# A hybrid decoder layer on one core: the first norm folded into the modulation rows, the sample output ahead of the routers, later ranks and normed rows behind the flags

## The reference, cut to what matters

```python
def hybrid_layer(x, c, ...):                     # 256 prompt tokens, and 8 x 8 sample tokens
    ada = jax.nn.silu(c) @ w_ada + b_ada
    shift1, scale1, gate1, shift2, scale2, gate2 = jnp.split(ada[:, None, :], 6, axis=-1)
    u = x * (1 + scale1) + shift1
    ...                                          # projection, attention or cache attention, short convolution
    mix = jnp.concatenate([attn, conv], axis=-1) @ w_o
    x = layer_norm(DEEPNORM_ALPHA * x + (1 + gate1) * mix, ln1_g, ln1_b)
    u2 = x * (1 + scale2) + shift2
    ffn = moe(u2, ...)                           # router on u2, top 4 of 32 experts, clamped SwiGLU
    x = layer_norm(DEEPNORM_ALPHA * x + (1 + gate2) * ffn, ln2_g, ln2_b)
```

## Time and profile before

| | us |
|---|---|
| median of three runs | 1467.15 (1466.29 to 1475.74) |
| the profiled execution's own time | 1470.0 |
| its span, first to last instruction | 1468.2 |
| PE busy, DVE busy, ACT busy in the span | 1390.4, 492.4, 243.8 |

### The profile page before, as it was taken

How to read it: one execution, slowest core, us unless ns; L and a number is a source line. 1 busy time by engine, 2 the same in 40 slices (tenths; PEclk the granted TensorE clock), 3 DMA queues, 4 the chain that set the end, 5 groups by cost and what they waited for, 6 DMA issues and landing times.

```text
span 1468.2 us, 21691 instructions
## 1 busy us (share of the span) xinstructions
PE 1390.4 (95%) x7813; PEld 574.1 (39%) x7814; DVE 492.4 (34%) x1098; ACT 243.8 (17%) x432; POOL 13.7 (1%) x22
## 2 busy tenths in 40 slices
PE   5999999999958999999999999999999999999993
PEld 2555666665432333333333333333333333333331
DVE  2211356554672222233223332223322322223336
ACT  0001334442010111111111111111111111111110
POOL 0000000000010000000000000000000000000000
PEclk9999999999968999999999999999999999999996
DMA  9949448999845889999999998999999999998941
GB/s 339 391 163 351 175 178 306 419 424 384 282 177 233 322 350 404 426 425 426 425 426 427 427 400 354 412 425 427 426 423 428 425 426 425 426 406 342 403 206 36
DMA packets 60900, 523.72 MB, mean 357 GB/s; under 512 B 8124, under 2 KB 8437, under 8 KB 20682
## 3 DMA queue, kind: packets, MB, share of 16 engines
q1 hardware_dynamic: 57696, 517.61, 86.0%
q0 software_dynamic: 1344, 4.90, 0.9%
q10 hardware_dynamic: 1834, 0.84, 0.3%
HBM read 519.87 MB, written 3.46 MB: 356 GB/s over the span
## 4 chain that ended last, share of the span: by engine, by line
PE 82%; DMA 10%; DVE 4%; issue 1%; SPq 1%; ACT 0%; DVEq 0%; ACTq 0%
PE ps L1679 29%; PE ps L1758 14%; PE ps L1280 6%; PE ps L1217 5%; PE ps L1584 5%; PE ps L1616 5%; DMA arena<-in_cache_v 4%; DMA arena<-in_w_up 4%; PE ps L1508 3%; DMA arena<-in_w_in 2%; PE ps L1671 2%; PE ps L1450 2%; PE ps L1277 2%; PE ps L1689 1%; PE ps L1607 1%
## 5 line engine op out<-in xcount | busy, mean ns | idle before, releaser
L1679 PE MATMUL ps<-arena 128*64 128x512 f32 x2048 | 450.5, 597 | 1.3 <-DMA arena<-in_w_up 1.2
L1679 PEld LDWEIGHTS ps<-arena 128*64 128x64 f32 x2048 | 144.3, 138 | 306.0 <-issue 302.4
L1758 PE MATMUL ps<-arena 128*64 128x512 f32 x1024 | 228.4, 599 | 2.4 <-issue 2.2
L1217 PE MATMUL ps<-arena 128*128 128x128 f32 (+4 forms) x1075 | 151.4, 282 | 30.9 <-DVEq L984 10.9
L1151 DVE TENSOR_SCALAR arena<-ps 128x512 f32<-128x512 f32 (+1 forms) x35 | 24.2, 692 | 417.6 <-PE ps L1679 356.4
L1217 PEld LDWEIGHTS ps<-arena 128*128 128x128 f32 (+4 forms) x1075 | 116.8, 144 | 94.1 <-issue 45.2
L1758 PEld LDWEIGHTS ps<-arena 128*64 128x64 f32 x1024 | 71.3, 138 | 153.8 <-issue 153.8
L1584 PE MATMUL ps<-arena 128*64 128x512 f32 (+1 forms) x396 | 97.5, 611 | 2.3 <-DVE arena L1092 2.3
L675 ACT ACTIVATE arena<-arena 128x512 f32<-128x512 f32 (+1 forms) x35 | 22.1, 631 | 446.5 <-DVE arena L1151 446.5
L1105 DVE TENSOR_TENSOR arena<-arena,ps 128x512 f32<-128x512 f32 x33 | 22.8, 690 | 196.3 <-PE ps L1607 196.0
L1280 PE MATMUL ps<-arena 128*128 128x320 f32 x288 | 85.0, 448 | 3.6 <-DMA arena<-in_w_in 3.6
(11 more groups left out here) (234 smaller groups left out, 900.9 us busy)
## 6 DMA issues: line engine op xcount, KB each, us to landing
arena<-in_w_up SPq DMA_DIRECT2D x128, 2048.0 KB, 15.2
arena<-in_w_down SPq DMA_DIRECT2D x128, 1024.0 KB, 12.7
arena<-in_w_ada SPq DMA_DIRECT2D x12, 2048.0 KB, 17.7
arena<-in_cache_k SPq DMA_DIRECT2D x16, 1536.0 KB, 14.3
arena<-in_cache_v SPq DMA_DIRECT2D x16, 1536.0 KB, 9.7
arena<-in_w_in SPq DMA_DIRECT2D x6, 2048.0 KB, 20.8
arena<-in_cache_k SPq DMA_DIRECT2D x32, 192.0 KB, 13.0
arena<-in_cache_v SPq DMA_DIRECT2D x32, 192.0 KB, 10.8
```

The costliest lines, as they stand in the source:

```text
L1217: return nc.tensor.transpose(o, i, ident[0:n, 0:n])
L1679: ins = mm(bank(part)[64 * h:64 * h + 64], xe_t[:, 0, at:at + 64], up_w[:, k, FF * part + 512 * h:FF * part + 512 * h + 512], start=False, ...
L1758: ins = mm(bank(3)[64 * h:64 * h + 64], a_t[:, 0, at:at + 64], dn_w[:, kk, 512 * h:512 * h + 512], start=kk == 0, stop=kk == KC - 1)
```

## The change

The first norm's gain and bias are multiplied into the modulation rows beforehand (`fold_norm`: shift2 + (1 + scale2) b, and (1 + scale2) g), for the prompt's rows ahead of `residual_sums(0)` and for the samples' behind `modulate(0)`. u2 then comes from the residual rows in two operations, through `mix`; the normed rows themselves are made by `keep_rows`, tiles 0 and 1 behind the flags, tile 2 behind the first `gathered_turned`. mod_s is loaded earlier, x for tile 2 later, the ln1 bias into the first eighth of w_down's place, whose last quarter to load now waits for `x1_kept`, as GpSimd's ln2 loads do; b_up is loaded after `wo_done` 3. `output_sample` stands ahead of router 0, the residual of tile 2 ahead of all routes, and the roots ahead of the exponentials on ScalarE. The gates are written by one operation. Ranks count from one (compared with `place`, which is iota + 1), and the later rounds' ranks are made behind the flags. Left out below: semaphore names, the places of `place`, `head_mask` and `query_sum`, and a separate bank for each tile's logits. Lines stand eight columns further left than in the file.

```diff
@@ -123,9 +122,7 @@
 MX = KTX + AC * NCACHE
-head_mask = view(MX, 256)
-query_sum = view(MX + 256, 3, 8)
-assert MX + 280 <= 24576
+assert MX <= 24576
@@ -213,7 +213,7 @@
 u2_t = view(R4 + 3 * D, KC, 128)
-ln1 = [view(R5, D), view(R2 + 2 * D, D)]
+ln1 = [view(R5, D), view(W + 16 * D, D)]
 xe_t = view(R4, 2, 512)
@@ -426,10 +427,10 @@
     sp.wait_ge(og_ready, 1)
-    for a, name in enumerate(("ln1_g", "ln1_b")):
-        sp.dma_start(ln1[a], t[name][0:1, :].to_broadcast([128, D])).then_inc(tail_in, 16)
+    sp.dma_start(ln1[0], t["ln1_g"][0:1, :].to_broadcast([128, D])).then_inc(ln1_in, 16)
     sp.wait_ge(vec_out, 64)
     sp.wait_ge(s_done, NB)
+    sp.dma_start(ln1[1], t["ln1_b"][0:1, :].to_broadcast([128, D])).then_inc(ln1_in, 16)
     sp.dma_start(mod_p, vectors[0:1, 0:3 * D].to_broadcast([128, 3 * D]).rearrange("p (a b) -> p a b", a=3)
@@ -437,22 +438,24 @@
     sp.dma_start(x1[:, 1, :], t["x_prompt"][0, 128:256, :]).then_inc(x_late, 16)
-    sp.dma_start(x1[0:64, 2, :], t["x_sample"].rearrange("b s d -> (b s) d")).then_inc(x_late, 16)
+    for b in range(NB):
+        src = vectors[1 + b:2 + b, 0:3 * D].to_broadcast([NS, 3 * D]).rearrange("p (a b) -> p a b", a=3)
+        sp.dma_start(mod_s[NS * b:NS * b + NS], src).then_inc(mod_late, 16)
     sp.wait_ge(v_used, NB)
...
     sp.wait_ge(so_copied, NB)
-    for b in range(NB):
-        src = vectors[1 + b:2 + b, 0:3 * D].to_broadcast([NS, 3 * D]).rearrange("p (a b) -> p a b", a=3)
-        sp.dma_start(mod_s[NS * b:NS * b + NS], src).then_inc(mod_late, 16)
+    sp.dma_start(x1[0:64, 2, :], t["x_sample"].rearrange("b s d -> (b s) d")).then_inc(x_late, 16)
     for m in range(2, KC // 2):
         sp.dma_start(up_w[:, 2 * m:2 * m + 2, :], wup_d[0, m]).then_inc(up_in[m], 16)
-    for m in range(KC // 2):
-        if m == 1:
-            sp.wait_ge(u2_ready, 3)
+    sp.wait_ge(wo_done, 3)
+    load_expert(0, None)
+    sp.wait_ge(u2_ready, 3)
+    for m in (1, 2, 3, 0):
+        if m == 0:
+            sp.wait_ge(x1_kept, 1)
         sp.dma_start(dn_w[:, 2 * m:2 * m + 2, :], wdn_d[0, m]).then_inc(dn_in[m], 16)
     sp.wait_ge(route_ready, 1)
-    load_expert(0, None)
     items = sp.value_load(flag_i[0:1, 0:1], min_val=NE, max_val=ITEMS)
@@ -505,6 +508,7 @@
     nc.gpsimd.memset(sel_t, 0.0).then_inc(cleared, 1)
+    pool.wait_ge(x1_kept, 1)
     for a, name in enumerate(("ln2_g", "ln2_b")):
@@ -643,8 +647,8 @@
-    for step, tt in ((act_root, 0), (act_norm, 1), (act_turn, 0), (act_root, 1), (act_exp, 0), (act_turn, 1),
-                     (act_root, 2), (act_exp, 1), (act_turn, 2), (act_exp, 2)):
+    for step, tt in ((act_root, 0), (act_norm, 1), (act_root, 1), (act_turn, 0), (act_root, 2), (act_turn, 1),
+                     (act_exp, 0), (act_turn, 2), (act_exp, 1), (act_exp, 2)):
         step(tt)
@@ -910,6 +914,9 @@
     V(v_.memset(qbd, 0.0))
+    v_.memset(gate_t[:, :, ITEMS:ITEMS + 1], 0.0)
+    V(v_.tensor_scalar(place, iota, 1.0, None, ALU.add))
+    V(v_.memset(place[:, CAP:128], -0.5))
@@ -962,26 +969,43 @@
             V(ins)
-        dve.wait_ge(tail_in, 48)
+        dve.wait_ge(tail_in, 16)
         if tt:
...
         V(v_.scalar_tensor_tensor(x_t, x_t, ALPHA, m, ALU.mult, ALU.add))
-        norm_sums(V, v_, x_t, n, st, var_ready)
+        norm_sums(V, v_, x_t, n, st, 50 + 4 * tt, var_ready)
+    def fold_norm(mod, n):
+        part = mix[0:n, 1, :]
+        V(v_.scalar_tensor_tensor(part, mod[0:n, 2, :], 1.0, ln1[1][0:n, :], ALU.add, ALU.mult))
+        V(v_.tensor_tensor(mod[0:n, 1, :], mod[0:n, 1, :], part, ALU.add))
+        V(v_.scalar_tensor_tensor(mod[0:n, 2, :], mod[0:n, 2, :], 1.0, ln1[0][0:n, :], ALU.add, ALU.mult))
...
-        n = TILES[tt][1]
+        n, mv = TILES[tt][1], 50 + 4 * tt
+        mod = mod_p if tt < 2 else mod_s
+        dve.wait_ge(sd_ready, (2, 4, 5)[tt])
+        V(v_.reciprocal(st[0:n, mv + 2:mv + 3], st[0:n, 36:37]))
+        V(v_.scalar_tensor_tensor(mix[0:n, tt % 2, :], x1[0:n, tt, :], st[0:n, mv:mv + 1], mod[0:n, 2, :],
+                                  ALU.subtract, ALU.mult))
+    def modulate(tt):
+        n, mv = TILES[tt][1], 50 + 4 * tt
+        mod = mod_p if tt < 2 else mod_s
+        V(v_.scalar_tensor_tensor(u2[0:n, tt, :], mix[0:n, tt % 2, :], st[0:n, mv + 2:mv + 3], mod[0:n, 1, :],
+                                  ALU.mult, ALU.add))
+        dve.sem_inc(u2_ready, 1)
+    def keep_rows(tt):
+        n, mv = TILES[tt][1], 50 + 4 * tt
         x_t = x1[0:n, tt, :]
-        norm_rows(dve, V, v_, x_t, n, st, ln1, sd_ready, (2, 4, 5)[tt], x_t)
-    def modulate(tt):
-        n = TILES[tt][1]
-        x_t, mod = x1[0:n, tt, :], mod_p if tt < 2 else mod_s
-        V(v_.scalar_tensor_tensor(u2[0:n, tt, :], mod[0:n, 2, :], 1.0, x_t, ALU.add, ALU.mult))
-        V(v_.tensor_tensor(u2[0:n, tt, :], u2[0:n, tt, :], mod[0:n, 1, :], ALU.add))
-        dve.sem_inc(u2_ready, 1)
+        V(v_.scalar_tensor_tensor(x_t, x_t, st[0:n, mv:mv + 1], ln1[0][0:n, :], ALU.subtract, ALU.mult))
+        V(v_.scalar_tensor_tensor(x_t, x_t, st[0:n, mv + 2:mv + 3], ln1[1][0:n, :], ALU.mult, ALU.add))
@@ -1028,9 +1052,15 @@
     dve_batch(NB - 1, False, False)
+    dve.wait_ge(ln1_in, 32)
+    dve.wait_ge(mod_in, 16)
+    fold_norm(mod_p, 128)
     residual_sums(0)
...
     mask_output(NB - 1)
+    modulate(0)
+    dve.wait_ge(mod_late, 128)
+    fold_norm(mod_s, 64)
     keep_output(NB - 1)
@@ -1038,7 +1068,6 @@
     squares(1)
-    modulate(0)
     mean_squares(1)
@@ -1059,24 +1088,24 @@
         V(v_.reciprocal(st[0:n, 41:42], st[0:n, 41:42]))
-        for r in range(ROUNDS):
-            v_.tensor_scalar(gate_t[0:n, tt, NE * r:NE * r + NE], ex[0:n, :], st[0:n, 41:42], None, ALU.mult)
-        V(v_.memset(gate_t[0:n, tt, ITEMS:ITEMS + 1], 0.0))
+        V(v_.tensor_scalar(gate_t[0:n, tt, 0:ITEMS].rearrange("p (r e) -> p r e", r=ROUNDS),
+                           ex[0:n, :].unsqueeze(1).to_broadcast([n, ROUNDS, NE]), st[0:n, 41:42], None, ALU.mult))
...
         n, rank_ps = TILES[tt][1], bank(3, NE * tt, NE * tt + NE) if tt < 2 else bank(2, 0, NE)
-        mk, rk = mask_t[0:n, tt, :], rank_t[0:n, tt, :]
-        V(v_.scalar_tensor_tensor(rk[:, 0:NE], rank_ps[0:n], FAR, mk, ALU.add, ALU.mult))
-        V(v_.tensor_scalar(rk[:, 0:NE], rk[:, 0:NE], -FAR, None, ALU.add))
+        V(v_.scalar_tensor_tensor(rank_t[0:n, tt, 0:NE], rank_ps[0:n], 1.0, mask_t[0:n, tt, :], ALU.add, ALU.mult))
+    def later_rounds(tt):
+        n, rk = TILES[tt][1], rank_t[0:TILES[tt][1], tt, :]
         for r in range(1, ROUNDS):
             v_.tensor_scalar(rk[:, NE * r:NE * r + NE], rk[:, 0:NE], -float(CAP) * r, None, ALU.add)
-        V(v_.memset(rk[:, ITEMS:ITEMS + 1], -FAR))
-    for step, tt in ((residual, 1), (route, 0), (residual, 2), (route, 1)):
+        V(v_.memset(rk[:, ITEMS:ITEMS + 1], 0.0))
+    for step, tt in ((residual, 1), (residual, 2), (route, 0), (route, 1)):
         step(tt)
     dve.sem_inc(masks_ready, 1)
-    V(v_.memset(iota[:, CAP:128], -0.5))
     route(2)
@@ -1089,12 +1118,12 @@
             if which == "sel":
-                ins = v_.tensor_scalar(sel[0:n, tt, :], iota[0:n, 0:CAP], rank_t[0:n, tt, bass.ds(i, 1)], None,
+                ins = v_.tensor_scalar(sel[0:n, tt, :], place[0:n, 0:CAP], rank_t[0:n, tt, bass.ds(i, 1)], None,
                                        ALU.is_equal)
...
                     sel_g[0:n, tt].rearrange("p (v d) s -> p v d s", v=2),
-                    iota[0:n, :].rearrange("p (v s) -> p v s", v=2).unsqueeze(2).to_broadcast([n, 2, 2, 64]),
+                    place[0:n, :].rearrange("p (v s) -> p v s", v=2).unsqueeze(2).to_broadcast([n, 2, 2, 64]),
                     rank_t[0:n, tt, bass.ds(i, 1)], gate_t[0:n, tt, bass.ds(i, 1)], ALU.is_equal, ALU.mult)
@@ -1124,6 +1153,10 @@
     dve.sem_inc(route_ready, 1)
+    for tt in range(3):
+        later_rounds(tt)
+    keep_rows(0)
+    keep_rows(1)
@@ -1132,6 +1165,8 @@
     gathered_turned(2, 1)
+    keep_rows(2)
+    dve.sem_inc(x1_kept, 1)
     dve.wait_ge(acc_ready, 1)
@@ -1530,18 +1565,18 @@
         pe.wait_ge(u2t_ready, 2 * tt + 2)
-        lg_ps = bank(5, NE * tt, NE * tt + NE)[0:n]
+        lg_ps = bank(LOGITS[tt], 0, NE)[0:n]
         for k in range(KC):
...
-    output(1, 1, range(4))
+    output(1, 1, range(2))
     sums_of_squares(1)
-    output(1, 1, range(4, KC)).then_inc(wo_done, 1)
+    output(1, 1, range(2, KC)).then_inc(wo_done, 1)
+    pe.wait_ge(og_ready, 2)
+    output_sample()
     pe.wait_ge(var_ready, 3)
     router(0)
-    pe.wait_ge(og_ready, 2)
-    output_sample()
     router(1)
@@ -1826,13 +1861,13 @@
-def norm_sums(V, v_, x, n, st, var_ready):
+def norm_sums(V, v_, x, n, st, mv, var_ready):
...
     V(ins)
-    V(v_.bn_aggr(st[0:n, 32:34], st[0:n, 20:32]))
-    v_.tensor_scalar(st[0:n, 35:36], st[0:n, 33:34], LN_EPS, None, ALU.add).then_inc(var_ready, 1)
+    V(v_.bn_aggr(st[0:n, mv:mv + 2], st[0:n, 20:32]))
+    v_.tensor_scalar(st[0:n, 35:36], st[0:n, mv + 1:mv + 2], LN_EPS, None, ALU.add).then_inc(var_ready, 1)
```

13 lines of the change are left out of this document (8 added, 5 removed).

## The result

| | before | after |
|---|---|---|
| median of the runs | 1474.44 us (6 runs, 1466.29 to 1480.12) | 1459.77 us (6 runs, 1456.06 to 1461.78) |
| ratio after / before | | 0.9922, 95% interval 0.9893 to 0.9952 |
| profiled execution, its span | 1470.0, 1468.2 us | 1456.86, 1455.1 us |
| mean granted clock of TensorE | 0.973 | 0.978 |

By the ratio that is 11.5 us of the 1474.44; the two medians themselves lie 14.67 us apart. The median of before was 1467.15 in the three runs that the forecast started from, 1474.44 in these six, and 1470.09 in seventeen later ones (1466.36 to 1476.03): so the ratio says more than the difference to any one median.

A forecast was written before the change was run, and what follows sets the result against it. TensorE was taken to bound the expert loop, VectorE the stretch ahead of its start. Gains of 5.0 + 2.4 + 1.4 + 0.7 + 0.8 = 10.3, less 0.5, left 9.8 us: 1457.3 us, range 1453.5 to 1462.5.

The forecast's parts named there:

- The time: Whole kernel: profiled span 1468.2 less 9.8 is 1460.2 us; runs' median 1457.3 us, or -0.7%.
- Within: Whole kernel: the measured time differs from before by no more than 1% (14.7 us); chance 0.90.
- Part 1: Norm and modulation of tiles 1 and 2: the fold takes 2.5 us per tile off VectorE's path, 5.0 in all.
- Part 2: Tile 0's route: moving GpSimd's memset of acc ends the stall of a VectorE tensor_scalar, gain 2.4 us.
- two-input operations would collide with the memset: Rival at tile 2's residual: the memset holds VectorE for 2.65 us, giving 1460.0 us; chance 0.04.
- Part 3: Gates and ranks ahead of the choice: gains of 1.4 for gates, 0.7 for memset and waits, 0.8 for ranks.
- Part 4: TensorE's order, sample output ahead of router 0: tile 2's residual and the logits come without a wait, no cost.
- Part 5: Behind the flags: later rounds and kept rows make VectorE late by 0.5 us for the copy, leaving 9.8 us gain.
- The clock: First expert's matmuls: the same clock loss of 2.9 us as before; bounds -2.9 and +2.
- The clock stays up: Rival at the first expert: TensorE's clock stays high and the expert is 2.9 us shorter, 1454.4 us; chance 0.14.
- The DMA sets the loop's end: Rival at the expert loop: 2.1 MB moved to its start cost 4.9 us, giving 1462.2 us; chance 0.10.
- The sample's x is late: Rival at tile 1's residual: x lands 10.6 us late and holds everything behind it, 1467.9 us; chance 0.03.

The follow-up runs named there:

- e5: The changed kernel once more, file unaltered, timed against the kernel before: 1458.58 us, ratio 0.9927.
- e2: The changed kernel with the kept rows of tiles 1 and 2 made right behind their modulation, not postponed: 1470.98 us, one run.
- e1: The kernel before, with only GpSimd's memsets of acc and y_sb moved behind the routes: 1467.52 us, one run.
- e4: The changed kernel with the old order: router 0 ahead of the sample output, tile 0's route between the residuals, roots between exponentials: 1461.96 us, one run.
- e6: The changed kernel with gates written by four operations and a memset, and the old ranks with later rounds ahead of the choice: 1460.46 us, one run.
- e3: The changed kernel with the kept rows of tiles 0 and 1 also moved behind the first copies of the turned gather: 1456.85 us, one run.

## Why the prediction was right or wrong

The mechanism and its size were right; what it was said to amount to was wrong.

- **The step that failed** stands at the end of "The time": -0.7%, "within the 1% (14.7 us) that a measurement of this kernel can tell from no change". Six runs against six put the ratio at 0.9922 with an interval of 0.3% on either side, and e5 with 6 against 11 at 0.9927 with 0.24%. A change of 0.7% is told from none here, twice. The 1% was taken over without a look at the spread of the three runs shown, 9.5 us or 0.64% from end to end: the median of some more runs is known far better than that. With the chance of 0.90 for "Within" the text called its own 9.8 us invisible. They are visible.
- **The size.** Forecast -9.8 us for the profiled execution's stretch, measured -9.7 at the up product; -11.5 by the first ratio and -10.7 by e5's. The 1457.3 lies 2.5 below the measured median of 1459.77 although the forecast gain is the smaller one: the 1467.15 that it was taken from lay low in what before can do (1466 to 1480). That the two nearly meet is in part luck.
- **Part 1** (5.0): right in amount. The kept rows behind the flags are worth 5.17 (e2): the fold without them takes no operation off the path. The loads of mod_s were taken too short. They were put at 4 to 7 us, and at 3.7 by half of 426 GB/s; their packets run from 370.25 to 379.55 in after, 9.3 us, and in before, in the row of 203 GB/s, from 388.85 to 398.56, where the loads of w_up ran among them. So that row's rate did not measure them. Where they ran nearly alone, the DMA engines had a share of 0.50, as eight of 16 would have, but moved 101 GB/s, a quarter of 426:

```profile
372.00:376.00 4.00, 4.00 (x57) 2.11 (x51) 3.86 (x6) 0.00 (x0) 0.00 (x0) 1.00 0.50 101
```

  The sample fold waited 1.07 us for them, inside the bounds of 0 to 1.2 and just beyond the 1 us named as a sign; nothing on the path behind it was late.
- **Part 2** (2.4): the size is right, 2.39 in e1. The way to it that was named, the order, is one of two that each suffice; the shorter residual is the other (e4). That two-input operations would collide with the memset is refuted: GpSimd's timeline of after has the memset beside the rows of tile 2's residual (1.39 and 1.22 us above, as in before).

```profile
399.97 2.65 POOL L506 MEMSET arena<- 128x3072 f32 x1 [199.41 <-PE ps L1495]
```

- **Part 3** (2.9 with memset and waits): right, 2.37 for gates and ranks in e6; the wait for the third logits is gone, and tile 2's rank waited 0.67 where some 1 us was named.
- **Part 4** (no cost): right. Tile 2's residual began at 400.49, 7.57 behind tile 1's (7.45 forecast), and the third logits were there 1.9 us before they were read. The sum to the choice, 10.3, measured 10.19.
- **Part 5** (VectorE late by 0.5): right in kind. From the end of the choice VectorE took 8.93 us to the copy (8.9 forecast), and the loss from gather to copy is 10.19 - 9.70 = 0.49; it would be about 0.8 (e3) had the gather not taken 4.46 instead of 4.83. What the step had not seen is how thin the margin is to TensorE: in e1, e2 and e6 the gather ran at 5.35 to 5.59 us and gave back up to all of what the part had gained.
- **The clock** (same loss): near. The first up product took 16.15, not 16.83, and the down product 7.09, not 8.67; 2.1 us that were only in the bounds. The windows of after show the level at 0.50 in 412 to 416 and again in 432 to 436, around the ranks and around the bias products with their gap:

```profile
412.00:416.00 4.00, 2.11 (x12) 1.89 (x11) 3.39 (x18) 0.32 (x1) 0.00 (x0) 0.50 1.01 426
...
424.00:428.00 4.00, 2.32 (x29) 1.06 (x19) 3.89 (x4) 1.28 (x3) 0.00 (x0) 1.00 0.00 0
...
432.00:436.00 4.00, 3.17 (x7) 0.82 (x8) 1.59 (x6) 0.00 (x0) 0.79 (x2) 0.50 0.83 301
...
440.00:444.00 4.00, 4.00 (x22) 1.39 (x20) 0.00 (x0) 0.00 (x0) 0.00 (x0) 1.00 0.60 168
```

  Counted from the first up product, the full clock came back in 438 to 440 in after, 3.3 to 5.3 us behind its start, and in 450 to 452 in before, 4.4 to 6.4 us behind. And in before it fell once more behind the gap ahead of the down product (472 to 475), in after it did not (461 to 465). In this order, after and before by turns:

```profile
438.00:440.00 2.00, 2.00 (x10) 0.61 (x8) 0.00 (x0) 0.00 (x0) 0.00 (x0) 0.70 0.42 162
450.00:452.00 2.00, 2.00 (x10) 0.57 (x8) 0.00 (x0) 0.00 (x0) 0.00 (x0) 0.64 0.00 0
461.00:465.00 4.00, 4.00 (x20) 1.34 (x18) 0.00 (x0) 0.00 (x0) 0.00 (x0) 1.00 0.53 176
472.00:475.00 3.00, 2.89 (x8) 1.02 (x10) 0.48 (x1) 0.00 (x0) 0.00 (x0) 0.50 0.55 229
```

- **The rivals.** "The clock stays up" is right in most of its 2.9 us (2.1) and not in its mechanism: the clock fell twice on the way to the loop, and 1.6 of the 2.1 stand in the down product. "The DMA sets the loop's end" fell: 986.03 us against 986.12. "The sample's x is late" fell: it landed 8.2 us after its issue at 384.5, and VectorE did not wait for it. Tile 1's residual did wait, 1.90 us, but for TensorE's product and not for x, so the sign "if VectorE waits in tile 1's residual" says nothing against the forecast.

## What to carry to other kernels

Before saying that a gain can't be measured, look at how far the runs already shown lie apart and how many there will be; a threshold that was given for something else is no measurement. A time that leaves one engine's list is only worth what the next engine's pace lets through: with TensorE in thin work its own clock gave back all of 2.4 us (e1), so read its granted clock where the gain is to arrive. And where an engine stands still with no semaphore behind it, look at the queue of the kind `instruction` in that stretch. Where two edits each remove the same collision, count it once, and undo them one at a time and together.
